# Layer 0's projection: the head sums of squares as two float32r products, with VectorE making the low half

## What is computed

```python
qkv = jax.nn.silu(short_conv(qkv, conv_w))
q, k, v = jnp.split(qkv, [GDN_QK_W, 2 * GDN_QK_W], axis=-1)
def l2norm(x):
    xf = x.astype(jnp.float32)
    return (xf * lax.rsqrt(jnp.sum(xf * xf, axis=-1, keepdims=True) + EPS)).astype(x.dtype)
```

## Time and profile before

| | |
|---|---|
| median of 3 runs | 4451.6 us (4450.91 to 4453.27) |
| profiled execution, its own time | 4466.34 us |
| its span, first to last instruction | 4464.6 us |
| mean granted TensorE clock | 0.955 of full speed |
| busy share of the span | PE 92%, PEld 76%, DVE 54%, ACT 51%, POOL 46% |
| the projection of layer 0 | about 240 to 1600 us of the span |

### The profile page before, as it was taken

How to read it: one execution, slowest core, us unless ns; L and a number is a source line. 1 busy time by engine, 2 the same in 40 slices (tenths; PEclk the granted TensorE clock), 3 DMA queues, 4 the chain that set the end, 5 groups by cost and what they waited for, 6 DMA issues and landing times. The chain is left out here.

```text
span 4464.6 us, 81760 instructions
## 1 busy us (share of the span) xinstructions
PE 4088.2 (92%) x30756; PEld 3414.3 (76%) x30756; DVE 2413.5 (54%) x2947; ACT 2288.2 (51%) x4486; POOL 2060.2 (46%) x1527
## 2 busy tenths in 40 slices
PE   7689999999999969999999999988999599978879
PEld 2378788778778858888888888876888488866657
DVE  3234544544544546666666666656665433248853
ACT  3345655655655646666666666652111511148831
POOL 1245565555556547777777777743111421200022
PEclk8899999999999979999999999999999699998889
DMA  5345555555455566666666666654443322355145
GB/s 221 99 129 158 148 159 157 147 154 158 144 157 160 152 187 197 198 198 197 201 197 199 199 198 198 200 164 182 180 188 127 100 108 114 131 206 202 76 140 138
DMA packets 777427, 733.30 MB, mean 164 GB/s; under 512 B 111904, under 2 KB 703264, under 8 KB 760416
## 3 DMA queue, kind: packets, MB, share of 16 engines
q1 hardware_dynamic: 684032, 681.48, 49.0%
q10 hardware_dynamic: 93056, 47.19, 3.5%
HBM read 483.12 MB, written 245.33 MB: 163 GB/s over the span
## 5 line engine op out<-in xcount | busy, mean ns | idle before, releaser
L610 PE MATMUL pj_bank<-h_hi,pj_whi 128*128 128x512 f32 (+1 forms) x1920 | 726.9, 379 | 14.5 <-POOL pj_first L596 14.5
L610 PE MATMUL pj_bank<-h_lo,pj_whi 128*128 128x512 f32 (+1 forms) x1920 | 707.6, 369 | 0.0
L1472 DVE TENSOR_TENSOR dc_Y<-dc_psY,dc_pick 128x256 f16<-128x256 f32 x864 | 326.1, 419 | 278.6 <-PE dc_psY L1261 278.6
L1398 ACT ACTIVATE dc_R<-dc_psE 128x256 f16<-128x256 f32 x864 | 285.0, 381 | 373.0 <-PE dc_psE L1275 372.8
L977 DVE RECIPROCAL pj_acc<-pj_acc 128x2304 f32<-128x2304 f32 x16 | 232.8, 14553 | 380.6 <-ACT pj_acc L883 380.6
L610 PEld LDWEIGHTS pj_bank<-h_hi,pj_whi 128*128 128x128 f32 x1920 | 363.4, 189 | 81.9 <-POOL pj_first L596 15.0
L914 ACT ACTIVATE pj_E<-pj_E,pj_gi 128x128 f32<-128x128 f32 x576 | 183.9, 392 | 464.0 <-DMA pj_gi<-scratch_gates 463.9
L610 PEld LDWEIGHTS pj_bank<-h_lo,pj_whi 128*128 128x128 f32 x1920 | 363.1, 189 | 66.5 <-issue 8.9
L766 POOL TENSOR_TENSOR pj_BD<-pj_E,pj_gi 128x512 f32<-128x512 f32 x144 | 158.6, 1101 | 549.1 <-ACT pj_E L917 549.1
L1190 POOL TENSOR_TENSOR dc_A<-dc_Lhi,dc_id 128x512 f16<-128x512 f16 x144 | 166.3, 1155 | 415.7 <-ACT dc_Lhi L1389 415.7
L610 PE MATMUL pj_bank<-h_hi,pj_first 128*128 128x512 f32 (+1 forms) x960 | 353.7, 368 | 0.0
(11 more groups left out here) (282 smaller groups left out, 10775.9 us busy)
## 6 DMA issues: line engine op xcount, KB each, us to landing
dc_dd<-scratch_decays SPq DMA_DIRECT2D x288, 256.0 KB, 5.5
dc_tm<-scratch_tm SPq DMA_DIRECT2D x288, 192.0 KB, 2.5
pj_E<-scratch_cgrow SPq DMA_DIRECT2D x288, 128.0 KB, 3.7
scratch_decays<-pj_E SPq DMA_DIRECT2D x144, 256.0 KB, 3.8
scratch_decays<-pj_BD SPq DMA_DIRECT2D x144, 256.0 KB, 3.8
dc_fm<-scratch_fm SPq DMA_DIRECT2D x288, 128.0 KB, 3.3
dc_egr<-scratch_egrow SPq DMA_DIRECT2D x288, 128.0 KB, 3.6
scratch_o<-dc_ob SPq DMA_DIRECT2D x288, 128.0 KB, 3.3
```

The costliest lines, as they stand in the source:

```text
L610: i = pe.matmul(self.bank[blk][:, 0:n], l[b][:, k, :], r[:, k, at:at + n], start=(m == 0), stop=(m == 3 * KT - 1))
L1398: act.activation(all_cols(R[q][p], l, True), split4(quart(bE[p]), l), ACT.Copy).then_inc(eR[p], 1)
L1472: dve.tensor_tensor(all_cols(Y[l - 1][p], l, True), split4(quart(bY[p]), l), split4(pick[:, l - 1].rearrange("p c t -> p (c t)"), l), ALU. ...
```

## The change

`acc` and `tm` get a second name of type float32r, and `ones_r` is a float32r name for the place of `ones`. ACT writes the square as float32r, that is rounded (`sq_hi`). DVE, ahead of `normalise` in each z stage, makes the square itself in float32 in the place of `tm`, waits for ACT's rounded one, and subtracts: the rest, rounded, is `sq_lo`. PE waits for both, and for each block multiplies ones by the high and by the low half in two float32r products that add up in one bank. Once at the start DVE rewrites the ones as float32r, and PE waits for that ahead of its first product. Three semaphores are new.

```diff
+    T["ones_r"] = nc.alloc_sbuf_tensor_at("ones_r", [P, P], F32R, offset=nc.sbuf_base - 4 * (1 + 12 * KT + P))
...
-        acc = sb("acc", [P, CONV])
+        acc, acc_r = raw_under(nc, ctx, "pj_acc", [P, CONV])
...
-        tm = sb("tm", [P, NCH, P])
+        tm, tm_r = raw_under(nc, ctx, "pj_tm", [P, NCH, P])
...
+        sq, sq_lo = (t[:].rearrange("p c t -> p (c t)") for t in (tm, tm_r))
+        sq_hi, ones_r = acc_r[:, 0:TOK], T["ones_r"][:]
...
                         pe.wait_ge(s["square"], nth(h, j, "qk"))
+                        pe.wait_ge(s["sq_lo"], nth(h, j, "qk"))
...
-                        pe.matmul(aux[b % 3][:, 0:n], T["ones"][:], acc[:, at:at + n], start=True, stop=True
+                        pe.matmul(aux[b % 3][:, 0:n], ones_r, sq_hi[:, at:at + n], start=True, stop=False)
+                        pe.matmul(aux[b % 3][:, 0:n], ones_r, sq_lo[:, at:at + n], start=False, stop=True
                                   ).then_inc(s["aux"], 1)
...
+                pe.wait_ge(s["ones"], 1)
                 sweep(stage)
...
-                        act.activation(acc[:, 0:TOK], act_row[:], ACT.Square).then_inc(s["square"], 1)
+                        act.activation(sq_hi, act_row[:], ACT.Square).then_inc(s["square"], 1)
...
+                dve.tensor_copy(ones_r, T["ones"][:]).then_inc(s["ones"], 1)
...
+                def square_low(h, j):
+                    n = nth(h, j, "qk")
+                    dve.wait_ge(s["silu"], nth(h, j, "qkv"))
+                    if h:
+                        dve.wait_ge(s["tm_out"], 16 * nth(h - 1, V1, "kv"))
+                    dve.tensor_tensor(sq, act_row[:], act_row[:], ALU.mult).then_inc(s["plain"], 1)
+                    dve.wait_ge(s["plain"], n)
+                    dve.wait_ge(s["square"], n)
+                    dve.tensor_tensor(sq_lo, sq, sq_hi.bitcast(F32), ALU.subtract).then_inc(s["sq_lo"], 1)
...
                 def stage(h, j, first):
                     if KINDS[j] == "z":
+                        square_low(h, j - 1)
                         normalise(h, j - 1)
```

More of the change, by code:

```diff
@@ L655, in phase_project_gdn @@
         names = ("const", "conv0", "conv1", "conv2", "conv", "pads", "silu", "square", "aux", "aux_read", "recip", "norm",
-                 "fm_out", "tm_out", "z_out", "fm_turn", "sides", "mask", "d_abs", "d_exp", "d_scaled", "d_done")
+                 "fm_out", "tm_out", "z_out", "fm_turn", "sides", "mask", "ones", "plain", "sq_lo", "d_abs", "d_exp", "d_scaled", "d_done")
         s = {q: sem("pj_" + q) for q in names}
```

## The result

The changed kernel took 4475.35 us, the median of six runs (4465.33 to 4479.55), against 4452.44 before (4446.9 to 4455.44, six runs): a ratio of 1.0051, interval 1.0040 to 1.0062, or 23 us more. In a second set of runs it was 4476.64 against 4452.03, ratio 1.0059 (1.0045 to 1.0073). The forecast was 4475, "slower".

The account below looks back on a forecast made before the run. It took PE's stream of products and the loop of decay, of nearly one length, to bound the kernel side by side. 4466.3 + 24 (15 distances x 1.3 = 20, plus 3.8 at the end) = 4490, less 14.7: 4475 us; range 4452 to 4510.

Parts of the forecast that it names:

- The products: On PE at each norm, two float32r products per block save 1.8 us, 29 us in 16.
- The low half: DVE's result, awaited by PE, comes 7.35 us behind the square's start, held up by POOL's subtraction of 2.35 us.
- The waits and the clock: PE waits some 50 us at the norms; the clock falls in all 16, +1.7 us where there was none.
- The distances: Between squares of layer 0's projection: 81.9 us grows by 1.3 each, 20 in 15, plus 3.8 behind the last norm.
- its own stream, at full clock, takes 79.9: PE's work between two squares without waits and clock losses, 2.0 us less than the distance of 81.9.
- the loop as a rival "alone": Loop of decay (load, ACT, POOL, store) alone sets the pace; only the end moves, +5, 4457 us; chance 0.16.
- PE's need of 2.65 + 2.0: In each distance PE would need 2.65 us beyond 81.9 plus its 2.0 to spare, set against the loop of decay.
- What gives back half of PE's lag: Silu waits for the convolution while POOL goes ahead with its split, shortening DVE's wait: x + x = 2.65, x = 1.3 us.
- 2.6 as the most: At a norm, PE can't come later than 2.6 us behind the square's start.
- every wait paid in full: Rival: ACT's roots or the convolution carry PE's lag into the loop of decay; +72, 4523 us; chance 0.15.
- The saved products win: Rival: PE reaches the norm more than 7.35 us behind the square's start, nothing waits; 4414 us; chance 0.09.
- POOL out of the way: Rival: POOL doesn't hold DVE up, low half at 5.25 us; +8 and +2 at the end, 4462 us; chance 0.08.

Follow-up runs that it names:

- e3: Changed kernel with the old float32 product of the unrounded square, low half still made and awaited: 4498.7 us, ratio 1.0102.
- e6: Changed kernel with POOL's split moved behind the second piece of decay in z stages: 4459.7 us, ratio 1.0009.
- e8: Kernel before without the third product of each slice in both projections: 4316.5 us, ratio 0.9689.
- e9: Kernel before with a shorter loop of decay (E masked and stored first, separate store semaphores), nothing left out: 4424.2 us, ratio 0.9936.
- e4: Changed kernel with PE's two parts of the sums moved back by one block: 4454.9 us, ratio 1.0004.

## Why the prediction was right, point by point

- **The size and the sign** came out: +23 against +24. The steps up to PE's waits held; the step from the waits to the distances was partly wrong, and that the sum still fits is partly luck.
- **The products** save what the trace of before said. At full clock the products of a norm follow each other at 0.12 and 0.23 (346.77 to 346.89 and to 347.12); e3, which has the old ones, is 22 to 23 us slower than the changed kernel.
- **The low half** comes at 7.3 to 7.5 us in 13 norms, for 7.35 forecast, and by the mechanism named: one engine stands until the other has finished. e6, which takes POOL's split away from there, brings 5.2. The multiplication of a tile by itself is held up like one of two tiles: by the Trainium skill (SBUF — State Buffer, "Who interferes with whom") two SBUF inputs of a DVE instruction exclude a GpSimd instruction that reads SBUF, and the traces agree for one tile named twice (4.77 against 2.56).
- **The waits and the clock:** 52.8 us for "some 50". The fall came at 14 norms for "all 16", and some at more than 1.7 us, so that the sum is the 16 x 1.7 = 27 us of the forecast; the second trace has 11 falls and 18 us. That the sum fits in the first is luck.
- **The distances:** I forecast 83.2 and the traces have 82.5 and 82.1; at the end +2.6 for +3.8. The step that was off is "its own stream, at full clock, takes 79.9", and that this stream binds with the convolution. What binds in the kernel before is the loop of decay and what hangs on it, at some 81 us (e8), by itself. And the 79.9 is too long. I took only the waits for the squares out of the 81.9, but from 283 to 1512 us PE also waited 8.4 us at the transposes, of which this row has most:

```profile
PE pj_aux L815 <- ACT pj_row L870: 6.4, 8, 1.9
```

  Without these 8.4 / 15 = 0.56 us the stream is 79.3, and e9, where PE waits 2.1 us in all, has 79.2. With 79.3 the forecast's own sum gives 79.3 - 1.8 + 1.7 + 4.75 = 83.95, half of the 2.05 above 81.9 for each distance, and some +19 us in place of +24. I had seen the loop as a rival "alone" and priced it at 4457, because I set PE's need of 2.65 + 2.0 against a fixed distance. What the traces show is that each distance goes by whichever comes last. In e8 it varies from 110 to 115 us from a k to the next q, and the square stands at its least distance behind the convolution's end, 4.39 us, in 5 of 16 norms; in the kernel before in 5 and 7, in the changed kernel in 13 of both traces. So PE with its longer wait passes the loop in most norms and not in all.
- **What gives back half of PE's lag** was named in the wrong place. I had POOL go ahead with its split. That is seen in two norms of 16. In most others it is the convolution: PE is late, and so is the convolution, and by then POOL has done its piece of decay. The timeline of the changed kernel at the three steps of one convolution, which run while POOL is idle:

```profile
833.97 7.94 DVE L1012 SCALAR_TENSOR_TENSOR pj_acc_raw<-pj_raw,pj_conv_w,pj_acc_raw 128x2307 f32<-128x2307 f32 x3
```

  7.94 / 3 = 2.65 us for one, where the mean before was 3118 ns (the same group on the page of before; 3094 in its second trace). Over the phase the mean of the changed kernel fell to 2824 ns, and to 2895 in its second trace:

```profile
L1012 DVE SCALAR_TENSOR_TENSOR pj_acc_raw<-pj_raw,pj_conv_w,pj_acc_raw 128x2307 f32<-128x2307 f32 x96 | 271.1, 2824 | 3.4
```

  With it silu comes earlier against PE, and PE reaches the norm up to 4.61 us behind the square's start where I took 2.6 as the most. The 2.6 was the reading of one trace: the second of the unaltered kernel has 3.6 twice. The wait then is 7.46 - 4.61 = 2.85 us, shown as 2.69 or 2.70 because the modelled ends hide 0.16; that stands in four of the 16 norms. The traces show +15 us and the runs +23; my sum of +24 hit the runs, and whether it would have been too high or just right with both steps mended, the traces can't say.
- **The rivals:** "every wait paid in full" (+72) is out. "The saved products win" is out for the reason given: no PE came 7.35 us late. "POOL out of the way" was built as e6 and gave +6 by the medians, for +10 forecast.

## What to carry to other kernels

Find the pace of a phase by taking work away from the engine that seems to bind, not from its busy share: here a third of the stream of a TensorE that is busy 98% of the phase could go and the squares stayed 81.2 us apart. A saving on an engine beside a loop that binds is worth nothing, while a wait added to it costs as soon as the two meet; so put the wait where the engine comes late anyway (e4 wins some 20 us back), or shorten the loop first (e9: 29 us from two semaphores split in two and two instructions swapped). Before work with two SBUF inputs goes to an idle VectorE, look at what GpSimd does in that very stretch.

## What was not expected of the hardware

- When DVE's multiplication ended and its subtraction followed 0.03 us later, POOL's waiting instruction went first each time, in four norms of the first trace and three of the second (846.55 for 4.59 us, then DVE's for 4.64). In these seven the engine with two such operations in a row didn't keep its turn.
- Two executions of one kernel differ by 14 us in this phase alone (1357.2 and 1343.4 us from the first split to the last store, before the change), while all else together agrees within 0.3 us. Two things in the phase aren't fixed by the order of instructions: when DMAs land, and whether the clock falls. In one trace of the changed kernel the same 2.69 or 2.70 us of idle was followed by a fall at 683 and 1025 us and by none at 347 and 1530. Which of the two makes the 14 us was not tried.
